# Gate chains inside the input projections, modulation beside a norm, pre-norm highs half by ScalarE, layer norms in two passes

## The reference

```python
# fox: 16 heads, forget gates
q, k, v, f = split(h @ w_in); log_f = log_sigmoid(f + b_f); c = cumsum(log_f)
logits[t, s] = q[t].k[s] / 8 + c[t] - c[s]            # for s <= t
# third block, per layer
mod = silu(c) @ ada_w[layer] + ada_b[layer]           # 6 x 1024
shift1, scale1, gate1, shift2, scale2, gate2 = split(mod)
hn = rmsnorm(x, norm1_w) * (1 + scale1) + shift1
x = x + gate1 * mixer(hn)                             # likewise with 2 and the feed-forward
# mlstm: i_pre = 15 tanh((i + i_bias) / 15), lf = log_sigmoid(f + f_bias), cumulated
```

## Time and profile before

| | |
|---|---|
| median of 3 runs | 3511.36 us (3511.13 to 3512.55) |
| the profiled execution, its own time | 3513.14 us |
| its span | 3511.3 us |
| mean granted TensorE clock | 0.94 |
| fox projection to attention | 1794.0 to 1818.2 us |
| modulation stage | 2090.6 to 2104.6 us |
| mLSTM projection to attention | 2181.4 to 2203.5 us |

### The profile page before, as it was taken

The page is one execution under the profiler, slowest core; times in us unless marked ns, Lnnn a source line. Parts: engine busy times, 40 slices in busy tenths (PEclk is TensorE's granted clock), DMA queues, the critical chain, the costliest instruction groups (busy, mean ns, idle before and its releaser), DMA issues. The chain is left out here.

```text
span 3511.3 us, 50762 instructions
## 1 busy us (share of the span) xinstructions
PE 3151.2 (90%) x20540; PEld 2793.7 (80%) x20540; DVE 2112.7 (60%) x3274; ACT 1367.8 (39%) x1919; POOL 101.6 (3%) x127
## 2 busy tenths in 40 slices
PE   7897999899999978789887989799866999999998
PEld 6896866689999966579766977589855899999997
DVE  5465698566666662766555656565467556555555
ACT  3443314444444432544434434343432333333332
POOL 0000000000000001000000000000021000000000
PEclk9998999999999988899988999699988899999999
DMA  6343588756666543045423543145511355555553
GB/s 264 135 184 142 192 347 349 265 197 210 211 211 212 189 172 122 25 144 190 157 73 120 181 158 141 36 162 180 198 49 54 126 183 192 180 183 192 181 182 123
DMA packets 71986, 598.21 MB, mean 170 GB/s; under 512 B 5552, under 2 KB 30640, under 8 KB 33200
## 3 DMA queue, kind: packets, MB, share of 16 engines
q1 hardware_dynamic: 44784, 571.26, 44.2%
q10 hardware_dynamic: 27072, 25.17, 2.2%
HBM read 582.78 MB, written 13.63 MB: 170 GB/s over the span
## 5 line engine op out<-in xcount | busy, mean ns | idle before, releaser
L1167 PE MATMUL ps<-x_hi,up_hi 128*128 128x256 f32 x3040 | 860.4, 283 | 9.3 <-DVE up_lo L1258 8.9
L1170 PE MATMUL ps<-x_lo,up_hi 128*128 128x256 f32 x3040 | 858.7, 282 | 0.0
L1171 PE MATMUL ps<-x_hi,up_lo 128*128 128x256 f32 x3040 | 858.6, 282 | 0.0
L1167 PEld LDWEIGHTS ps<-x_hi,up_hi 128*128 128x128 f32 x3040 | 581.7, 191 | 23.4 <-DVE up_lo L1258 10.4
L1170 PEld LDWEIGHTS ps<-x_lo,up_hi 128*128 128x128 f32 x3040 | 581.9, 191 | 10.1
L1171 PEld LDWEIGHTS ps<-x_hi,up_lo 128*128 128x128 f32 x3040 | 581.8, 191 | 0.0
L1258 DVE TENSOR_TENSOR up_lo<-ring,up_hi 128x1024 fp32r<-128x1024 f32 (+1 forms) x270 | 447.1, 1656 | 37.2 <-ACT up_hi L1214 26.9
L333 DVE TENSOR_TENSOR weight_lo<-ring,weight_hi 128x1024 fp32r<-128x1024 f32 x236 | 288.6, 1235 | 261.1 <-ACT weight_hi L326 252.7
L1263 DVE TENSOR_TENSOR down_lo<-ring,down_hi 128x1024 fp32r<-128x1024 f32 x270 | 330.1, 1223 | 167.9 <-ACT down_hi L1220 167.9
L1188 PE MATMUL ps<-down_lo,hidden_hi 128*128 128x512 f32 x1080 | 423.9, 392 | 0.0
L1184 PE MATMUL ps<-down_hi,hidden_hi 128*128 128x512 f32 x1080 | 421.6, 390 | 0.0
(11 more groups left out here) (435 smaller groups left out, 4237.2 us busy)
## 6 DMA issues: line engine op xcount, KB each, us to landing
ring<-in_stream SPq DMA_DIRECT2D x181, 2048.0 KB, 7.8
ring<-in_stream SPq DMA_DIRECT2D x110, 1536.0 KB, 6.4
gates<-kept_gates ACTq DMA_DIRECT2D x12, 1024.0 KB, 8.8
kept_gates<-away_first ACTq DMA_DIRECT2D x8, 768.0 KB, 10.8
kept_gates<-away_last ACTq DMA_DIRECT2D x8, 768.0 KB, 9.0
params_mix<-in_mix SPq DMA_DIRECT2D x1, 3072.0 KB, 21.6
params_ada<-in_ada SPq DMA_DIRECT2D x1, 2080.0 KB, 7.8
params_ln<-in_ln SPq DMA_DIRECT2D x2, 1024.0 KB, 5.2
```

Of the source, the lines that this page charges most:

```text
L1167: last = pe.matmul(out, hi[:, o:o + P], x_hi[:, k, :], start=(k == 0), stop=False)
L1170: pe.matmul(out, hi[:, o:o + P], x_lo[:, k, :], start=False, stop=False)
L1171: last = pe.matmul(out, lo[:, o:o + P], x_hi[:, k, :], start=False, stop=(k == DK - 1))
```

## The change

The gate chunks of fox and mLSTM move to the second place of their stream and projection. The gate biases are applied by ScalarE; Exp, Ln, Tanh, the scans, the repeats by `pick` and the masks take place while later chunks are multiplied, the repeats in between two products by token. Fox's separate repeat stage is gone, and its `pick` is made after the prologue. The modulation stage is gone: the adaptive biases are written into unused rows of `mod` by three transfers in the ln2 stage and `band_row` gets a second one per column, so that the selecting matmul adds them; the rows of layer 0, shifts and gains are made in the fox block's last `post_norm`, the gate rows of layer 1 in the SwiGLU's `add_gated`. ScalarE writes the high part of every second pre-norm block itself, reading PSUM once more. The layer norm subtracts the mean and applies the gain in one pass before the power arrives, and scales and adds the bias in a second.

```diff
     product(a["nsa_w_out_2"][0].reshape(16, HD, D)[order].reshape(D, D))
     mlp(a["mlp_w_up_2"][0], a["mlp_w_down_2"][0])
-    product(a["fox_w_in_2"][0])
+    w = a["fox_w_in_2"][0]
+    product(w[:, 0:WIDE])
+    product(w[:, 3 * D:])
+    product(w[:, WIDE:3 * D])
     product(a["fox_w_out_2"][0])
     mlp(a["mlp_w_up_2"][1], a["mlp_w_down_2"][1])
-    product(a["m_w_in_3"][0])
+    w = a["m_w_in_3"][0]
+    product(w[:, 0:WIDE])
+    product(w[:, 3 * D:])
+    product(w[:, WIDE:3 * D])
     product(a["m_w_out_3"][0])
     glu(a["ffn_w_gate_3"][0], a["ffn_w_up_3"][0], a["ffn_w_down_3"][0])
...
                 last = dve.bn_aggr(moments[:, t, :], stats[:, t, :, :].rearrange("p a b -> p (a b)"))
             step(last)
             dve.tensor_scalar(spare[:], moments[:, :, 1], LN_EPS, None, ALU.add).then_inc(var_ready, 1)
+            for t in range(TT):
+                last = dve.scalar_tensor_tensor(y[:, t, :], y[:, t, :], moments[:, t, 0:1], g, ALU.subtract, ALU.mult)
+            step(last)
             dve.wait_ge(rstd_ready, 1)
             for t in range(TT):
-                last = dve.tensor_scalar(y[:, t, :], y[:, t, :], moments[:, t, 0:1], rstd[:, t:t + 1],
-                                         ALU.subtract, ALU.mult)
-            step(last)
-            step(dve.tensor_tensor(y[:, :, :], y[:, :, :], spread(g, 1, TT), ALU.mult))
-            return dve.tensor_tensor(out[:, :, :], y[:, :, :], spread(b, 1, TT), ALU.add)
+                last = dve.scalar_tensor_tensor(out[:, t, :], y[:, t, :], rstd[:, t:t + 1], b, ALU.mult, ALU.add)
+            return last
...
                 for b in range(DK):
                     act.wait_ge(self.turned, b + 1)
+                    bias = 0.0 if self.bias is None else self.bias(b)
+                    if b % 2 == 0:
+                        act.activation(self.parts[0][:, b, :], ps[:, 4 + b % 4, 0:TOKENS], ACT.Identity, scale=self.gain(b),
+                                       bias=bias).then_inc(self.act_hi, 1)
                     act.activation(hT[:, b, :], ps[:, 4 + b % 4, 0:TOKENS], ACT.Identity, scale=self.gain(b),
-                                   bias=0.0 if self.bias is None else self.bias(b)).then_inc(self.turned_read, 1)
+                                   bias=bias).then_inc(self.turned_read, 1)
             def split(self, dve):
                 for b in range(DK):
                     dve.wait_ge(self.turned_read, b + 1)
-                    split_block(dve, hT, self.parts, b, self.part_hi, self.ready, b)
+                    if b % 2:
+                        split_block(dve, hT, self.parts, b, self.part_hi, self.ready, b // 2)
+                    else:
+                        dve.wait_ge(self.act_hi, b // 2 + 1)
+                        dve.tensor_tensor(self.parts[1][:, b, :], hT[:, b, :], self.parts[0][:, b, :],
+                                          ALU.subtract).then_inc(self.ready, 1)
...
                     sp.dma_start(buf_2[:], d["ln2"]).then_inc(params_loaded, 16)
+                    for g in range(ADA_ROWS // BIAS_ROWS):
+                        sp.dma_start(mod[g * BAND + ADA_ROWS:(g + 1) * BAND, :],
+                                     d["ada"][g * BIAS_ROWS:(g + 1) * BIAS_ROWS, :]).then_inc(bias_loaded, 16)
+                    sp.wait_ge(bias_loaded, 16 * (ADA_ROWS // BIAS_ROWS))
...
+                        if beside is not None:
+                            beside.keep(act, t)
+                        square_x(act, x_ready, junk, t)
...
                         mixer.power(pool)
                     token_powers(pool, var_ready, rstd_ready)
+                    if beside is not None:
+                        beside.gains(pool)
...
-                    weights = weight_parts("ttttnn.", sems[:len(PARTS)], own)
...
+                    norm = PreNorm(lambda b: col("norm_g", 2 * DK + b), x_parts, sems[len(PARTS):], own, xhat=v)
...
-                        at = 0
-                        for _ in range(4):
-                            at = parts_t(pe, weights, x_parts, at, t_ready, t_read, norm.ready if at == 0 else None)
-                        for n in range(2):
-                            parts_n(pe, weights, x_parts, n, n_ready, n_read)
-                        product_t(pe, hT, [(0, HEADS_B)], at, t_ready, t_read)
+                        at = parts_t(pe, weights, x_parts, 0, t_ready, t_read, norm.ready)
+                        at = product_t(pe, hT, [(0, HEADS_B)], at, t_ready, t_read)
+                        for _ in range(3):
+                            at = parts_t(pe, weights, x_parts, at, t_ready, t_read)
+                        parts_n(pe, weights, x_parts, 0, n_ready, n_read)
+                        pe.wait_ge(t_read, n_t)
...
+                        pe.wait_ge(pick_ready, 1)
+                        for n in range(pairs):
+                            if n == 3:
+                                pe.wait_ge(decay_copied, 1)
+                            if n >= 4:
+                                pe.wait_ge(repeated_read, n - 3)
+                            for b in range(2):
+                                last = pe.matmul(ps[:, n % 4, b * TOKENS:b * TOKENS + TOKENS], pick[:, 2 * n + b, :], forget[:, 2, :],
+                                                 start=True, stop=True)
+                            last.then_inc(repeated, 1)
+                        parts_n(pe, weights, x_parts, 1, n_ready, n_read)
...
+                        for at in range(n_t):
                             act.wait_ge(t_ready, at + 1)
+                            if at == 4:
+                                act.activation(forget[:, 0], ps[0:HEADS_B, 0, 0:TOKENS], ACT.Identity,
+                                               bias=col("b_f", rows=HEADS_B)).then_inc(t_read, 1)
+                                continue
...
+                            weights.high(act, b + 5)
+                            if at == 7:
+                                act.wait_ge(act_step, 1)
+                                act.activation(forget[:, 1], forget[:, 1], ACT.Exp, scale=-1.0).then_inc(act_step, 1)
+                                act.wait_ge(act_step, 2)
+                                act.activation(forget[:, 1], forget[:, 1], ACT.Ln, bias=1.0).then_inc(act_step, 1)
+                        weights.high(act, 23)
+                        act.wait_ge(turned, 1)
+                        act.activation(decay[:], ps[:, 3, 0:TT * HEADS_B].rearrange("p (t h) -> p t h", t=TT),
+                                       ACT.Copy).then_inc(decay_copied, 1)
                         weights.high(act, 24)
...
-                        for n in range(2):
-                            weights.low(dve, 23 + n)
-                            dve.wait_ge(n_ready, n + 1)
-                            dve.tensor_copy(v[:, :, n * WIDE:n * WIDE + WIDE], bank_n(n)).then_inc(n_read, 1)
-                        dve.wait_ge(t_ready, 17)
-                        step(dve.tensor_scalar(forget[:, 0], ps[0:HEADS_B, 0, 0:TOKENS], col("b_f", rows=HEADS_B), None, ALU.add))
+                        weights.low(dve, 7)
+                        dve.wait_ge(t_read, 5)
                         dve.scalar_tensor_tensor(forget[:, 1], forget[:, 0], -1.0, forget[:, 0], ALU.mult, ALU.max).then_inc(act_step, 1)
+                        weights.low(dve, 12)
                         dve.wait_ge(act_step, 3)
                         step(dve.scalar_tensor_tensor(forget[:, 0], forget[:, 0], 0.0, forget[:, 1], ALU.min, ALU.subtract))
                         dve.tensor_tensor_scan(forget[:, 2], ones[0:HEADS_B, :], forget[:, 0], 0.0, ALU.mult, ALU.add).then_inc(summed, 1)
...
+                        weights.low(dve, 23)
+                        for n in range(pairs):
...
+                        weights.low(dve, 24)
+                        for n in range(2):
+                            dve.wait_ge(n_ready, n + 1)
+                            dve.tensor_copy(v[:, :, n * WIDE:n * WIDE + WIDE], bank_n(n)).then_inc(n_read, 1)
+                    @block.gpsimd
+                    def _(pool):
+                        norm.power(pool)
+                        step = Chain(pool, pool_step)
+                        pool.wait_ge(norm.ready, DK)
+                        step(pool.memset(pick[:], 0.0))
+                        pool.affine_select(out=pick[:], in_=pick[:], compare_op=ALU.not_equal, fill=-1.0, base=0,
+                                           pattern=[[-1, HEADS_B], [0, P]], channel_multiplier=1).then_inc(pick_ready, 1)
...
+        class GateRows:
+            SIGNALS = ("repeated", "repeated_read")
+            def __init__(self, layer, gates):
+                self.rows = [layer * 12 + piece * 2 + half for piece in (2, 5) for half in range(2)]
+                self.gates = gates[:, layer * 2 * D:(layer + 1) * 2 * D].rearrange("p (n m) -> p n m", m=WIDE)
+            def begin(self, sems):
+                self.repeated, self.repeated_read = sems
+            def select(self, pe):
```

(81 more changed lines are left out.)

189 lines of the change are left out of this document (64 added, 125 removed).

## The result

The changed kernel takes 3475.68 us (median of 4 runs, 3474.08 to 3477.88). The kernel before, timed beside it, takes 3511.7. The ratio is 0.9898 (95% interval 0.988 to 0.9915), so it is faster by 36 us. Its profiled execution has a span of 3473.7 us against 3511.3, 37.6 less. The prediction was 3471.5 with a range of 3465 to 3479: sign and size hold, but several of its terms do not, and this part is mostly about them.

The account below looks back on a forecast made before the run. TensorE was busy 90% of the span, so only its idle or 1.2 GHz stretches pay. Terms 11.8, 7.2, 0.8, 13.6, 4.7, -0.7 and 2.5 sum to 39.9 us off the 3511.4 median: 3471.5 us, range 3465 to 3479.

Parts of the forecast that it names:

- Term 1: Fox gates: gate chain hidden inside the projection, repeat between the two v products at 7.0 us; net 11.8 us saved.
- Term 2: mLSTM gates: chain moved into the projection, with three table loads and a margin of 1.2 us; net 7.2 us saved.
- rival B: Gate chain late in the middle of a projection, costing 3 to 6 us: 3476 us, chance 0.10.
- Rival C: Each table switch holds ScalarE twice as long as the one load shows, lengthening the mLSTM chain: 3477 us, chance 0.03.
- Attention: Attention starts with TensorE at the high clock in fox and mLSTM: 0.8 us saved for both (0 to 2).
- Term 3: Modulation: its 14.0 us stage goes, the work hidden in the norm before it; net 13.6 us saved (11 to 14).
- rival D: Modulation isn't hidden: small products and copies stand before additions and squares, 3 us: 3474.5 us, chance 0.08.
- Term 4: Three layer norms, each with four passes of 1.24 us, two covering the power; net 4.7 us saved (3.5 to 6).
- Term 5: Pre-norm highs shared with ScalarE: small gains in some prologues, router losing 1.8 us; sum -0.7 us without fox.
- Term 6: Fox prologue: GpSimd's memset and select moved behind it, 3.4 us less 0.9 lost; net 2.5 us saved.
- rivals B to F: Alternatives to the main forecast (0.70); the one not named singly: attention keeps the high clock for several heads, 3465, chance 0.07.
- F: Slower than before: TensorE stays at 1.2 GHz to the end of both projections, +45 us: 3516 us, chance 0.02.

Follow-up runs that it names:

- e1: Changed kernel with the fox and mLSTM gate repeats made from 128 rows (zeros below the real ones) instead of 16 and 8: 3465.92 us.
- e7: Changed kernel with both gate chains behind the last product and the fox selecting matrix made early, as before the change: 3491.57 us.
- e5: Changed kernel, but GpSimd makes the fox selecting matrix at once, as before, not behind the prologue: 3477.53 us.
- e9: The joined version e8, but with all highs of all pre-norms on VectorE, as before the change: 3468.33 us.
- e6: Changed kernel with the three layer norms in three passes, as before the change: 3482.18 us.
- e4: Changed kernel, but in the router's pre-norm VectorE makes all the highs, as before the change: 3472.34 us.
- e10: The changed kernel again with no edit, profiled a second time: one time, 3477.0 us.
- e8: Changed kernel with the fox, mLSTM and router repeats from 128 rows and the router's highs on VectorE alone: 3459.2 us.

## Why the prediction was right, and where it was not

**Term 1, fox gates: 11.8 predicted, 6.6 measured** (7.35 with the first scores). The sum priced the repeat's 32 matmuls "like the mLSTM gate product, 7.07/32 = 0.221 each", on the ground that TensorE had been busy. That row was of matmuls with 128 rows; the repeat has 16. Price and place were right for TensorE at the high clock (e1: 11.5, or 12.25 with the first scores), but it does not keep it: 3.3 us in the repeat (10.45 - 7.17) and 1.6 behind it, which are the 4.9 us of e1. The 14.0 us that stood in brackets, for a low clock throughout, was the other bound. The kernel before had the same 32 matmuls at 0.437 us each, and the low clock of that stretch was put down to the waits of the chain alone. VectorE's masks did not pace it: the same masks follow the 7.17 us of e1.

**Term 2, mLSTM gates: 7.2 predicted, 6.7 measured**, 8.25 with full rows. Against e7, whose stretch behind the first block was 1.05 shorter than before's, they are 5.7 and 7.2. Here the same fall costs 1.5 us, and in e5, where it came earlier in the repeat (4.56 instead of 3.7 us), 3.3 (82.50 against e1's 79.23). The gate chain has only one table load, not three: Tanh and Exp start at 2108.58 and 2108.89, 0.31 apart, without one; only Ln has one, 1.28 us. The scan ends at 2116.4 and TensorE asks for it at 2121.3, so the margin is 4.9 us rather than 1.2, and rival B had even less chance than it was given. That Tanh shares a table with Exp is stated by the Trainium skill (ScalarE: Activation LUTs, Table sets: the hidden batching unit); the trace agrees, with no load between the two. Rival C falls with it: the activation behind the load starts 0.02 us after its end.

**Attention: 0.8 predicted for both stages; measured 3.0 in fox.** The first scores give the 0.7 that was worked out. The 2.3 behind them were not foreseen: the code is identical, and it took 71.04 to 72.52 us in nine of the ten profiles with early gates but 73.62 in e9, and with late ones 73.44 (e7) and 74.75 (before). How much of the 2.3 belongs to the gates and how much to the clock's phase is not settled. In mLSTM the step was wrong: the granted clock was 0.50 from 2162.7 to 2165.3 us, as its attention began, and the first four score matmuls took 0.81 us before and after.

**Term 3, modulation: 13.6 predicted, 13.6 measured** (211.01 to 197.38, with the feed-forward's prologue in it). The cover named was the right one; rival D did not come.

**Term 4, layer norms: 4.7 predicted, 6.4 measured** by the lengths of the three stages (e6's median, 6.5, agrees partly by chance, as said there). The up to 0.5 us that GpSimd's power might hold VectorE did not occur: the first two passes took 2.47 us for both tiles, as they would alone, and the power (1.67 us) ran beside them. And the first norm gave 2.17 us where its pause had been charged with 1.3.

**Term 5, highs: the router's -1.8 is exact** (e4). For the others e9 shows 0.8 us without fox, where the prediction had 1.1; hgrn's loss of 0.35 came out as 0.38. Prologues of the same code differ by as much as these terms (e9, e10), so the sum is not confirmed beyond its order.

**Term 6, fox prologue: 2.5 predicted, 3.3 measured.** The step that failed is the 0.9 us charged for memset and select beside the later weight lows. The timeline behind the prologue:

```profile
1717.44 2.35 DVE L337 TENSOR_TENSOR weight_lo<-ring,weight_hi 128x1024 fp32r<-128x1024 f32 x2
1719.53 2.13 POOL L2377 TENSOR_SCALAR_AFFINE_SELECT pick<-pick 16x2048 f32<-16x2048 f32 x1 [0.15 <-POOL pick L2376]
1719.71 3.03 DVE L337 TENSOR_TENSOR weight_lo<-ring,weight_hi 128x1024 fp32r<-128x1024 f32 x1
```

The two lows beside the memset (1717.59 to 1719.39) keep their length, 1.22 us each, overlapping by 0.1; the one beside the select takes 3.03 us instead of 1.22. That delay never reached TensorE: the stretch from the first q block to attention takes 84.31 us, and 84.26 in e5, where both stand in the prologue. The Trainium skill (SBUF — State Buffer, Who interferes with whom) had given 3.4 for this term. The trace agrees with both sides of its rule: the subtraction waits beside the select, which reads SBUF, and not beside the memset, which only writes it.

Terms 1 and 2 fell short of the forecast by 5.7 us, terms 4 and 6 and attention exceeded it by 4.7, and the banded attention gave 2.3 us in the first profile that no term has. With term 5 at -1.0 that makes some 41 us, and the spans differ by 37.6: the rest was lost again in stages that no edit touches. At 303 us, behind the second layer norm, the changed kernel is 5.9 us ahead of the one before, at 401 us only 2.9. The windows over the same work, the kernel before and then the changed one:

```profile
315.00:321.00 6.00, 5.16 (x16) 4.17 (x17) 5.83 (x13) 2.54 (x4) 0.00 (x0) 0.72 1.03 424
309.00:315.00 6.00, 4.75 (x11) 3.80 (x12) 5.86 (x12) 2.52 (x3) 0.00 (x0) 0.50 1.02 421
```

So the right total is in part luck: errors of terms cancel, and so do gains and losses from when the clock happens to be low. None of rivals B to F happened; F was nearest in kind, since TensorE did drop to 1.2 GHz in the projection. It did so for the second half of the repeat and 8 matmuls behind it, though, not to the end.

**Left open.** Most of e9's 7 us in stages it does not touch. In part of the runs TensorE's matmuls of the nsa projection start 0.118 us apart and in the others 0.113 on average, at granted clock 1.00 in both; no run here tells why. e8 is clearly faster than the changed kernel (3459.04 to 3464.57 against 3474.08 to 3477.88), but its 16 us contain perhaps 5 that another execution may not show. Between 32 and 64 rows no height was tried.

## What to carry to other kernels

Before you price a small matmul in the middle of dense ones, look at its operands' height: with 8, 16 or 32 rows a stretch of a few microseconds took the clock away from itself and from the product behind it, and rows of zeros up to 64 or 128 gave it back at no cost that the traces show. Sharing a copy between two engines pays only where the engine that gets more work isn't the one waited for: check each caller of a shared helper, since one line gained 0.5 us in one stage (fox, e9) and lost 1.8 in another (the router, e4). Judge effects of 1 to 3 us by the length of the edited stage in the trace, with one repeated profile of the same kernel to see what unedited stages do.
